# Even layer: the second heads' logarithms in one row on ScalarE, their operands at slab eleven, the sums over later keys one slab on, and two projections in borrowed PSUM banks

## The chip, the cores and the metric

The kernel runs on one core of one Trainium2 chip. The metric is the device time of one execution in microseconds (us); lower is better. It is compared as the median over several executions.

## The reference, cut to what matters

The program is two small networks in a row over 256 tokens of width 1024, all in float32. The first is one gated recurrent block with an expert layer. The second has two layers; each is an FFN, a mixer and an FFN with residuals. The mixer of the even layer is the stage that the change is about; the odd layer's mixer (16 heads over blocks of 256 keys) is touched in one place.

```python
def even_mixer(h, w_in, w_pool, pool_scale, w_out):
    proj = h @ w_in                                   # 1024 -> 2048
    q, k, v, u = jnp.split(proj, [512, 1024, 1536], axis=-1)
    a = stick_breaking_attention(q, k, v by 8 heads of 64)
    p = multiscale_pool(u, w_pool, pool_scale)
    return jnp.concatenate([merge_heads(a), p], axis=-1) @ w_out

# stick_breaking_attention, per head and block of 128 queries
z = q @ k.T / 8
past = spos < tpos
log_1m = where(past, log_sigmoid(-z), 0)
later = cumsum(log_1m, axis=keys, reverse=True) - log_1m
a = where(past, exp(log_sigmoid(z) + later), 0)
out = a @ v
```

In front of every FFN and mixer stands `rmsnorm`: x is divided by the root of its mean square per token and scaled by a gain.

## The kernel before

**Weights.** All weights come as one stream of slabs (128 x 1024 float32, 512 KB) through a ring of four buffers. Each slab passes three engines: SyncE loads `raw`, ScalarE rounds it to `w_hi` (`split_hi`, line 559), VectorE subtracts to get `w_lo` (`split_lo`, line 939). Slab n + 4 can be split only when TensorE has used slab n. TensorE multiplies every weight tile three times (hi x hi, lo x hi, hi x lo), so a slab is 24 matmuls.

**Norm.** The product of a projection is linear in x, so TensorE starts with the unscaled operand (`h_hi`, `h_lo`), and `rstd`, the reciprocal root, is multiplied in when a tile is read out. Its own chain is: squares, a matmul with ones (`norm`, PE), `Sqrt` (`root`, ScalarE), `RECIPROCAL` (line 962, VectorE). In `even_in` and `qkv`, `norm` is issued after slab 1.

**Projection.** `project` puts slab i of a stage into `tile_buf(j)`, which alternates between two buffers of the PSUM tensor `tile`. `free_tile(j)` makes PE wait until the reader of tile j - 2 (VectorE's `take`, or ScalarE) is done. So slab 2 of `even_in` and of `qkv` waits for the first `take`, and that one for `rstd`.

**Even layer.** `even_in` has 16 slabs. By a permutation of the stream, slabs 0 to 7 are q and k of a pair of heads each, 8 to 11 are the four groups of u for the pooling, and 12 to 15 are v, taken in pairs by `project_tokens` (48 matmuls each, slabs 12 and 13, then 14 and 15; the reader is ScalarE's `take_v`). The attention is done in two groups g of four heads:

- `head_scores(pair)` on PE, after slabs 3, 5, 7 and 8, writes z into `banks`, four PSUM banks that are FFN accumulators (`acc`) in other stages; ScalarE copies them to `az` (line 840).
- `ln_one_plus(g)` on ScalarE: Abs (814), Exp (816), Ln (818). Exp and Ln need different function tables, and each change of table is an `ACT_TABLE_LOAD`. Group 0 has its steps at slabs 5 and 6, group 1 at slabs 8, 9 and 10, one each, with a `split_hi` between.
- `stick_L_of(g)` on VectorE: `asp` (1469), the masked operand `aL` (1471) that PE waits for, `az - asp` (1474).
- `later_sums(g)` on PE: 16 matmul instructions, four heads into the four `banks`. Group 0 comes after slab 9, group 1 after slab 11. Group 1 writes the banks of group 0, so each of its heads waits until VectorE has read that of group 0 (`stick_w`).
- `stick_logs(g)` on VectorE (1481) reads those banks; `stick_exp(g)` on ScalarE (825) and `stick_shares(g)` on VectorE (1487) end with the weights `az`.
- `window_means(0..3)` on VectorE (1500 to 1505) is the pooling.

Each engine runs the order in which its own block of code is written. VectorE does, per slab, `take`, then `split_lo` of the slab four on. Before the `split_lo` of slab 12 + 4 it has one long block: logs of group 0, operands of group 1, shares of group 0, window means and logs of group 1 in turn. After the projections, PE multiplies the pooled values (it waits for the last `take_v`), forms the attention outputs, and starts `even_out` when `y_lo` is ready (`y`, line 1531, is the first step to it on VectorE).

**Odd layer.** `qkv` starts in the same way (slabs 0, 1, `norm`, slabs 2, 3, `turn_rstd`, `head_scores(0)`); its head scores use banks 0 and 1 only.

Of the kernel before, what the change touches and what calls it, by code (L numbers as in the profile page):

```python
# [29 lines left out]
T = 256  # L30
# [78 lines left out]
POOL_SLABS, EVEN_V = 8, 12  # L109
# [58 lines left out]
def build(nc, stream, x_in, cols_in, ones_in, keys_in, wpool_in, mixc_in, attc_in, out):  # L168
    first, NSLAB = stream_plan()
    readers = tile_readers(first)  # L170
    tile_at = {}
# [22 lines left out]

    def tile_buf(j, half=0):

        return tile[:, 2 * (j % 2) + half, :]

    def pair_buf(c, tt):
# [3 lines left out]
    def reads(engine, j):  # L203

        return sum(r == engine for r in readers[:j + 1])

    with ExitStack() as ctx:
# [109 lines left out]
        tile = ctx.enter_context(nc.psum_tensor("tile", [P, 4, T], F32))  # L317
        banks = acc[:, :, :].rearrange("p (b a) t -> p b (a t)", b=4)
        fronts = front[:, :, :]


        landed = [sem(f"slab_landed{i}") for i in range(RING)]
# [3 lines left out]
        slab_used = sem("slab_used")  # L326
        pool_done = sem("pool_products_done")
        tile_read = {"act": sem("tile_read_by_act"), "dve": sem("tile_read_by_dve")}
# [208 lines left out]
        def _(act):  # L537
# [247 lines left out]
            for kind, i in layer_stages():  # L785
# [21 lines left out]
                elif kind == "even":  # L807
                    def ln_one_plus(g, steps):

                        of = slice(4 * g, 4 * g + 4)  # L810
                        for step in steps:
                            if step == 0:
                                act.wait_ge(z_read, 4 * g + 4)
                                link(nc.scalar.activation(asp[:, of, :], az[:, of, :], ACT.Abs))
                            elif step == 1:
                                link(nc.scalar.activation(asp[:, of, :], asp[:, of, :], ACT.Exp, scale=-1.0))
                            else:
                                nc.scalar.activation(asp[:, of, :], asp[:, of, :], ACT.Ln, bias=1.0)\
                                    .then_inc(ln_ready, 1)

                    def stick_exp(g):

                        a, b = 4 * g, 4 * g + 4
                        act.wait_ge(stick_w, b)
                        nc.scalar.activation(az[:, a:b, :], az[:, a:b, :], ACT.Exp).then_inc(stick_e, 1)

                    n = first["even_in"]
                    for i in range(16):
                        if i == EVEN_V:
                            stick_exp(0)  # L830
                            stick_exp(1)
                        act.wait_ge(slab_used, n + i + 1)
                        if i >= EVEN_V and i % 2:
                            take_v("even_in", i - 1, i - 1 - EVEN_V, av)
                        split_hi(n + i + RING)
                        if i in STICK_AFTER:
                            pair = STICK_AFTER[i]
                            for h in (2 * pair, 2 * pair + 1):
                                act.wait_ge(z_done, h + 1)
                                nc.scalar.activation(az[:, h, :], banks[:, h % 4, 0:3 * P], ACT.Copy,  # L840
                                                     scale=SCALE).then_inc(z_read, 1)
                        if i == 5:
                            ln_one_plus(0, range(2))
                        elif i == 6:
                            ln_one_plus(0, [2])
                        elif i in (8, 9, 10):
                            ln_one_plus(1, [i - 8])
                    act.wait_ge(tile_read["dve"], reads("dve", tile_at["pooled"] + 3))
                    nc.scalar.copy(y_hi[:, 4:8, :], y32[:, 4:8, :]).then_inc(y_hi_ready, 1)
                    for g in range(2):  # L850
# [73 lines left out]
        def _(dve):  # L924
# [516 lines left out]
            for at, (kind, i) in enumerate(stages):  # L1441
# [18 lines left out]
                elif kind == "even":  # L1460
# [4 lines left out]
                    def stick_L_of(g):  # L1465

                        a, b = 4 * g, 4 * g + 4
                        dve.wait_ge(ln_ready, g + 1)
                        link(nc.vector.scalar_tensor_tensor(asp[:, a:b, :], az[:, a:b, :], 0.0,
                                                            asp[:, a:b, :], ALU.max, ALU.add))  # L1470
                        nc.vector.tensor_tensor(aL[:, a:b, :], asp[:, a:b, :],
                                                past_neg.unsqueeze(1).broadcast_to([P, 4, 3 * P]),
                                                ALU.mult).then_inc(stick_L, 1)
                        link(nc.vector.tensor_tensor(az[:, a:b, :], az[:, a:b, :], asp[:, a:b, :],
                                                     ALU.subtract))

                    def stick_logs(g):

                        for h in range(4 * g, 4 * g + 4):
                            dve.wait_ge(later_done, h + 1)  # L1480
                            nc.vector.tensor_tensor(az[:, h, :], banks[:, h % 4, 0:3 * P], az[:, h, :],
                                                    ALU.add).then_inc(stick_w, 1)

                    def stick_shares(g):
                        a, b = 4 * g, 4 * g + 4
                        dve.wait_ge(stick_e, g + 1)
                        nc.vector.scalar_tensor_tensor(az[:, a:b, :], az[:, a:b, :], -1.0,
                                                       past_neg.unsqueeze(1).broadcast_to([P, 4, 3 * P]),
                                                       ALU.mult, ALU.mult).then_inc(stick_a, 1)

                    def window_means(g):

                        src = pu[:, g, :]
                        if g == 0:
                            dve.wait_ge(tile_read["dve"], reads("dve", tile_at["even_in"] + POOL_SLABS + 3))
                        else:
                            dve.wait_ge(pooled_ready, g)
                        for r in range(g + 1):
                            to = win[:, r % 2, :]
                            link(nc.vector.tensor_tensor(to[:, PAD:], src[:, PAD:],  # L1500
                                                         src[:, PAD - 2 ** r:PAD - 2 ** r + T], ALU.add))
                            src = to
                        link(nc.vector.tensor_tensor(src[:, PAD:], src[:, PAD:], inv_count[:, g, :],
                                                     ALU.mult))
                        nc.vector.tensor_tensor(pooled[:, g, :], src[:, PAD:], pu[:, g, PAD:],
                                                ALU.subtract).then_inc(pooled_ready, 1)

                    n = first["even_in"]
                    for i in range(16):
                        if i == 4:  # L1510
                            r_columns(2)
                        if i < POOL_SLABS:
                            take("even_in", i, (ak if i % 2 else aq)[:, i // 2, :])
                        elif i < EVEN_V:
                            take("even_in", i, pu[:, i - POOL_SLABS, PAD:PAD + T])
                        if i == EVEN_V:
                            stick_logs(0)
                            stick_L_of(1)
                            stick_shares(0)
                            window_means(0)  # L1520
                            window_means(1)
                            stick_logs(1)
                            window_means(2)
                            stick_shares(1)
                            window_means(3)
                        split_lo(n + i + RING)
                        if i == 8:
                            stick_L_of(0)
                    dve.wait_ge(pool_done, 4)
                    for g in range(4):  # L1530
                        nc.vector.tensor_scalar(y32[:, 4 + g, :], tile[:, g, :],
# [85 lines left out]
        def _(pe):  # L1617
# [11 lines left out]
                return mm(out, lo, r_hi, False, stop, **kw)  # L1629

            def free_tile(j):
                if j >= 2:
                    r = readers[j - 2]
                    pe.wait_ge(tile_read[r], reads(r, j - 2))

            def project(name, i, n, hi, lo, lows=None, ks=range(KT), parts={}):

# [301 lines left out]
            for kind, i in layer_stages():  # L1939
# [5 lines left out]
                elif kind == "even":  # L1945
# [30 lines left out]
                    for i in range(16):  # L1976
                        if i < EVEN_V:
                            project("even_in", i, n + i, h_hi, h_lo, lows if i == 0 else None)
                        elif i % 2 == 0:
                            project_tokens("even_in", i, i - EVEN_V, n + i, h_hi, h_lo)  # L1980
                        if i == 1:
                            norm(q - 1)
                        elif i == 3:
                            turn_rstd(q - 1)
                        if i in STICK_AFTER:
                            head_scores(STICK_AFTER[i])
                        if i == 9:
                            later_sums(0)
                        elif i == 11:
                            later_sums(1)  # L1990
# [162 lines left out]
```

## Time and profile before

| | |
|---|---|
| median of 3 executions | 2194.0 us (2191.49 to 2195.93) |
| profiled execution, its own time | 2195.41 us |
| its span | 2193.4 us |
| busy in the span: PE / VectorE / ScalarE | 2059.9 (94%) / 1476.1 (67%) / 1079.0 us (49%) |
| mean granted TensorE clock | 0.977 |
| stage of the even mixer (`even_in` to the start of `even_out`) | 1363.3 to 1449.1 us |
| start of `qkv` to the start of `w_o` | 1861.4 to 1963.7 us |

The span is what the trace covers; the time of the execution is 2.0 us longer. The profiled execution lies 1.4 us above the median. A row of the timeline gives start and duration in us, engine, line, operation, and in brackets how long the engine had been idle and which instruction released it.

### The profile page before, as it was taken

Reading aid. Unit: us, or ns where it says so; the run is one execution under the profiler, and the core shown is the slowest. Engines: PE = TensorE matmul, PEld = TensorE weight load, DVE = VectorE, ACT = ScalarE, POOL = GpSimd, SP = SyncE. Lnnn points to the kernel's source line nnn. Section 1 sums busy time; section 2 is a strip of 40 time slices with the busy share of each in tenths; the row PEclk is TensorE's granted clock in tenths of the full one; section 3 lists DMA queues with packets and bytes.
Section 4 is the critical chain, followed back from the end, with each engine's and each line's share of the span. In section 5 each row is a group of like instructions: output and inputs, shape, how many; then the busy total and the mean of one; then the engine's idle time right before and its main releaser. Section 6 shows DMA issues by size and latency. Waiting matters only on the chain.

```text
span 2193.4 us, 42453 instructions
## 1 busy us (share of the span) xinstructions
PE 2059.9 (94%) x15492; PEld 1953.6 (89%) x15492; DVE 1476.1 (67%) x2393; ACT 1079.0 (49%) x1659; POOL 55.4 (3%) x36
## 2 busy tenths in 40 slices
PE   7899967899999999999998999799999999999997
PEld 7898865689999999999998999689999999889997
DVE  5687699966666666666666556676556556856555
ACT  5445326944444444444445444544445444555443
POOL 0000240000000000000000000000000000000000
PEclk9899998999999999999999999999999999999999
DMA  5344430045555555555555555335555565335552
GB/s 195 120 135 146 152 116 1 0 156 187 184 191 185 187 183 191 189 184 184 189 188 168 186 174 170 125 106 188 186 174 171 181 185 180 126 125 173 183 187 100
DMA packets 95683, 348.19 MB, mean 159 GB/s; under 512 B 10752, under 2 KB 10880, under 8 KB 95360
## 3 DMA queue, kind: packets, MB, share of 16 engines
q1 hardware_dynamic: 95184, 344.88, 48.3%
q10 hardware_dynamic: 432, 2.36, 0.3%
q8 instruction: 48, 0.79, 0.1%
q14 instruction: 19, 0.16, 0.0%
HBM read 346.15 MB, written 1.05 MB: 158 GB/s over the span
## 4 chain that ended last, share of the span: by engine, by line
PE 81%; DVE 12%; ACT 4%; issue 2%; DVEq 0%; DMA 0%; ACTq 0%; SPq 0%
PE front L1619 39%; PE acc L1619 29%; PE tile L1619 12%; DVE w_lo L939 2%; DVE pick L1392 2%; ACT w_hi L559 2%; DVE pick L1386 1%; DVE rstd L962 1%; DVE h_lo L969 1%; DVE chosen L1368 0%; DVE x L1450 0%; DVE rest L1283 0%; DVE top_i L1279 0%; DVE top_i L1297 0%; DVE top_v L1275 0%
## 5 line engine op out<-in xcount | busy, mean ns | idle before, releaser
L939 DVE TENSOR_TENSOR w_lo<-raw,w_hi 128x1024 fp32r<-128x1024 f32 x636 | 778.2, 1224 | 188.4 <-ACT w_hi L559 188.1
L559 ACT CAST w_hi<-raw 128x1024 fp32r<-128x1024 f32 x652 | 680.5, 1044 | 360.1 <-PE front L1619 144.4
L1619 PE MATMUL front<-h_hi,w_hi 128*128 128x256 f32 x2432 | 690.2, 284 | 8.2 <-DVE h_lo L969 7.5
L1619 PE MATMUL front<-h_hi,w_lo 128*128 128x256 f32 x2432 | 689.0, 283 | 0.0
L1619 PE MATMUL front<-h_lo,w_hi 128*128 128x256 f32 x2432 | 688.9, 283 | 0.0
L1619 PEld LDWEIGHTS front<-h_hi,w_hi 128*128 128x128 f32 x2432 | 466.9, 192 | 15.1 <-DVE h_lo L969 5.4
L1619 PEld LDWEIGHTS front<-h_lo,w_hi 128*128 128x128 f32 x2432 | 467.0, 192 | 5.0
L1619 PEld LDWEIGHTS front<-h_hi,w_lo 128*128 128x128 f32 x2432 | 467.0, 192 | 0.0
L608 ACT ACTIVATE scaled<-scaled 128x256 f32<-128x256 f32 x216 | 90.2, 418 | 500.6 <-DVE scaled L1024 289.0
L1019 DVE TENSOR_TENSOR scaled<-front,rstd 128x512 f32<-128x512 f32 x88 | 60.8, 691 | 275.9 <-PE front L1619 275.8
L1619 PE MATMUL tile<-h_hi,w_hi 128*128 128x256 f32 x736 | 219.8, 299 | 23.0 <-DVE h_lo L1082 4.9
L1619 PE MATMUL tile<-h_lo,w_hi 128*128 128x256 f32 x736 | 213.5, 290 | 0.0
L1619 PE MATMUL tile<-h_hi,w_lo 128*128 128x256 f32 x736 | 213.2, 290 | 0.0
L1619 PE MATMUL acc<-w_hi,mid_hi 128*128 128x512 f32 x512 | 201.9, 394 | 2.8 <-DVE mid_lo L1038 2.8
L1619 PE MATMUL acc<-mid_hi,w_hi 128*128 128x256 f32 x704 | 200.0, 284 | 4.2 <-DVE mid_lo L1038 4.2
L1619 PE MATMUL acc<-w_hi,mid_lo 128*128 128x512 f32 x512 | 201.3, 393 | 0.0
L1619 PE MATMUL acc<-w_lo,mid_hi 128*128 128x512 f32 x512 | 199.7, 390 | 0.0
L1619 PE MATMUL acc<-mid_lo,w_hi 128*128 128x256 f32 x704 | 199.3, 283 | 0.0
L1619 PE MATMUL acc<-mid_hi,w_lo 128*128 128x256 f32 x704 | 199.2, 283 | 0.0
L1619 PEld LDWEIGHTS tile<-h_hi,w_hi 128*128 128x128 f32 x736 | 146.5, 199 | 29.2 <-issue 7.8
L1619 PEld LDWEIGHTS tile<-h_lo,w_hi 128*128 128x128 f32 x736 | 146.8, 199 | 0.3 <-issue 0.2
L1619 PEld LDWEIGHTS tile<-h_hi,w_lo 128*128 128x128 f32 x736 | 146.5, 199 | 0.0
(254 smaller groups left out, 2622.0 us busy)
## 6 DMA issues: line engine op xcount, KB each, us to landing
raw<-stream SPq DMA_DIRECT2D x652, 512.0 KB, 3.5
x<-x_t SPq DMA_DIRECT2D x2, 512.0 KB, 4.8
keysT<-keys_t ACTq DMA_DIRECT2D x1, 1024.0 KB, 5.5
attc<-attention_constants ACTq DMA_DIRECT2D x1, 1024.0 KB, 5.6
out_t<-h SPq DMA_DIRECT2D x4, 256.0 KB, 2.2
mixc<-mixer_constants SPq DMA_DIRECT2D x1, 704.0 KB, 9.2
wpool<-w_pool ACTq DMA_DIRECT2D x1, 256.0 KB, 7.0
lane<-lanes SPq DMA_DIRECT2D x1, 128.0 KB, 4.8
```

The lines of the kernel that those rows point to most:

```text
L559: nc.scalar.copy(w_hi[:, s, :], raw[:, s, :]).then_inc(hi_ready, 1)
L608: nc.scalar.activation(scaled[:, k, 0:T], scaled[:, k, 0:T], func).then_inc(gate_ready, 1)
L939: nc.vector.tensor_tensor(w_lo[:, s, :], raw[:, s, :], w_hi[:, s, :].bitcast(F32), ALU.subtract).then_inc(lo_ready, 1)
L962: nc.vector.reciprocal(rstd[:, :], rstd[:, :]).then_inc(rstd_ready, 1)
L969: nc.vector.scalar_tensor_tensor(h_lo[:, k, :], x[:, k, :], col(gain, k), h_hi[:, k, :].bitcast(F32), ALU.mult, ALU.subtract)\
L1019: nc.vector.tensor_tensor(scaled[:, k, :].rearrange("p (a t) -> p a t", a=2), fronts[:, k, :].rearrange("p (a t) -> p a t", a=2), r, ALU.m ...
L1386: nc.vector.tensor_tensor(rows, iota.unsqueeze(1).broadcast_to([P, 3, P]), idx1_T[:, t(1, 3)].unsqueeze(2).broadcast_to([P, 3, P]), ALU.is ...
L1392: nc.vector.tensor_tensor(pick2[:, half, :, :], iota.unsqueeze(1).broadcast_to([P, 4, P]), idx2_T[:, t].unsqueeze(2).broadcast_to([P, 4, P ...
L1619: return nc.tensor.matmul(out, lhsT, rhs, start=start, stop=stop, **kw)
```

## The change

Five edits in one kernel:

1. In `even_in` and `qkv`, slabs 2 and 3 are projected into banks 2 and 3 of `banks` in place of `tile`, with no wait for a reader. Slabs 4 and 5, which use `tile` again, wait for the readers of slabs 0 and 1.
2. On ScalarE the three steps of `ln_one_plus(1)` all stand at slab 8, with no `split_hi` between.
3. On PE `later_sums(0)` comes after slab 10, not 9.
4. On VectorE `stick_L_of(1)` and then `stick_logs(0)` stand after the `split_lo` of turn 10 (slab 14), ahead of `take` of slab 11. In the block at slab 12 the order becomes means 0 and 1, shares 0, logs 1, means 2 and 3, shares 1.
5. On ScalarE `stick_exp(1)` is issued after the wait for slab 12, not before.

```diff
     def tile_buf(j, half=0):
+        for name in ("even_in", "qkv"):
+            if name in first and 2 <= j - tile_at[name] < 4:
+                return borrowed[j - tile_at[name]]
         return tile[:, 2 * (j % 2) + half, :]
...
+        borrowed = {i: banks[:, i, 0:T] for i in (2, 3)}
...
                         if i == EVEN_V:
                             stick_exp(0)
+                        act.wait_ge(slab_used, n + i + 1)
+                        if i == EVEN_V:
                             stick_exp(1)
-                        act.wait_ge(slab_used, n + i + 1)
...
-                        elif i in (8, 9, 10):
-                            ln_one_plus(1, [i - 8])
+                        elif i == 8:
+                            ln_one_plus(1, range(3))
...
                         if i == EVEN_V:
-                            stick_logs(0)
-                            stick_L_of(1)
-                            stick_shares(0)
                             window_means(0)
                             window_means(1)
+                            stick_shares(0)
                             stick_logs(1)
                             window_means(2)
+                            window_means(3)
                             stick_shares(1)
-                            window_means(3)
                         split_lo(n + i + RING)
                         if i == 8:
                             stick_L_of(0)
+                        elif i == 10:
+                            stick_L_of(1)
+                            stick_logs(0)
...
             def free_tile(j):
-                if j >= 2:
-                    r = readers[j - 2]
-                    pe.wait_ge(tile_read[r], reads(r, j - 2))
+                before = 2
+                for name in ("even_in", "qkv"):
+                    if name in first and 2 <= j - tile_at[name] < 4:
+                        return
+                    if name in first and 4 <= j - tile_at[name] < 6:
+                        before = 4
+                if j >= before:
+                    r = readers[j - before]
+                    pe.wait_ge(tile_read[r], reads(r, j - before))
...
-                        if i == 9:
+                        if i == 10:
                             later_sums(0)
                         elif i == 11:
                             later_sums(1)
```

**PE at the start of `even_in`.** The rows begin with `norm` (the matmul of `sq` with ones in `lane`); what follows is slab 2. Before, then of the change:

```order
L1619 MATMUL front<-sq,lane 128x256 [waits norm_squares_added]
L1619 MATMUL tile<-h_hi,w_hi 128x256 [waits slab_lo_ready,tile_read_by_dve]
L1619 MATMUL tile<-h_lo,w_hi 128x256
L1619 MATMUL tile<-h_hi,w_lo 128x256
L1619 MATMUL tile<-h_hi,w_hi 128x256
```

```order
L1625 MATMUL front<-sq,lane 128x256 [waits norm_squares_added]
L1625 MATMUL acc<-h_hi,w_hi 128x256 [waits slab_lo_ready]
L1625 MATMUL acc<-h_lo,w_hi 128x256
L1625 MATMUL acc<-h_hi,w_lo 128x256
L1625 MATMUL acc<-h_hi,w_hi 128x256
```

The target is now `acc`, and the wait for VectorE's reader is gone; the same holds for slab 3 and for both in `qkv`.

**VectorE from `take` of slab 9 on** (`pu` is u of the pooling). Before, then of the change:

```order
L991 TENSOR_TENSOR pu<-tile,rstd 128x256 [waits slab_used,dve_own_steps]
L939 TENSOR_TENSOR w_lo<-raw,w_hi 128x1024 [waits slab_hi_ready]
L991 TENSOR_TENSOR pu<-tile,rstd 128x256 [waits slab_used]
L939 TENSOR_TENSOR w_lo<-raw,w_hi 128x1024 [waits slab_hi_ready]
L991 TENSOR_TENSOR pu<-tile,rstd 128x256 [waits slab_used]
L939 TENSOR_TENSOR w_lo<-raw,w_hi 128x1024 [waits slab_hi_ready]
L1481 TENSOR_TENSOR az<-acc,az 128x384 [waits stick_later_done] x4
L1469 SCALAR_TENSOR_TENSOR asp<-az,asp 128x1536 [waits stick_ln_ready]
L1471 TENSOR_TENSOR aL<-asp,attc 128x1536 [waits dve_own_steps]
L1474 TENSOR_TENSOR az<-az,asp 128x1536
L1487 SCALAR_TENSOR_TENSOR az<-az,attc 128x1536 [waits stick_exp_ready,dve_own_steps]
```

```order
L996 TENSOR_TENSOR pu<-tile,rstd 128x256 [waits slab_used,dve_own_steps]
L944 TENSOR_TENSOR w_lo<-raw,w_hi 128x1024 [waits slab_hi_ready]
L996 TENSOR_TENSOR pu<-tile,rstd 128x256 [waits slab_used]
L944 TENSOR_TENSOR w_lo<-raw,w_hi 128x1024 [waits slab_hi_ready]
L1474 SCALAR_TENSOR_TENSOR asp<-az,asp 128x1536 [waits stick_ln_ready]
L1476 TENSOR_TENSOR aL<-asp,attc 128x1536 [waits dve_own_steps]
L1479 TENSOR_TENSOR az<-az,asp 128x1536
L1486 TENSOR_TENSOR az<-acc,az 128x384 [waits stick_later_done,dve_own_steps]
L1486 TENSOR_TENSOR az<-acc,az 128x384 [waits stick_later_done] x3
L996 TENSOR_TENSOR pu<-tile,rstd 128x256 [waits slab_used]
L944 TENSOR_TENSOR w_lo<-raw,w_hi 128x1024 [waits slab_hi_ready]
```

The operands `aL` and then the logs of group 0 have moved up by one `take` and one `split_lo`, and the logs now follow the operands.

**ScalarE from the Abs of group 1 on.** Before, then of the change:

```order
L814 ACTIVATE asp<-az 128x1536 [waits stick_z_read]
L559 CAST w_hi<-raw 128x1024 [waits slab_landed3,slab_used,act_own_steps]
L816 ACT_TABLE_LOAD
L816 ACTIVATE asp<-asp 128x1536
L559 CAST w_hi<-raw 128x1024 [waits slab_landed0,slab_used,act_own_steps]
L818 ACT_TABLE_LOAD
L818 ACTIVATE asp<-asp 128x1536
L559 CAST w_hi<-raw 128x1024 [waits slab_used,slab_landed1]
```

```order
L818 ACTIVATE asp<-az 128x1536 [waits stick_z_read]
L820 ACT_TABLE_LOAD
L820 ACTIVATE asp<-asp 128x1536 [waits act_own_steps]
L822 ACT_TABLE_LOAD
L822 ACTIVATE asp<-asp 128x1536 [waits act_own_steps]
L563 CAST w_hi<-raw 128x1024 [waits slab_used,slab_landed3]
L563 CAST w_hi<-raw 128x1024 [waits slab_used,slab_landed0]
L563 CAST w_hi<-raw 128x1024 [waits slab_used,slab_landed1]
```

The number of instructions and of table loads is the same; the casts of slabs 13 and 14, each of which waits for a slab to be used, now stand behind the Ln.

## Rows read from the trace of the kernel before

**Rows 1.** The page, section 4: chain that ended last, by engine

```profile
PE 81%; DVE 12%; ACT 4%; issue 2%; DVEq 0%; DMA 0%; ACTq 0%; SPq 0%
```

**Rows 2.** Timeline, TensorE alone: first matmuls after a pause

```profile
1374.76 0.39 PE L1619 MATMUL tile<-h_hi,w_hi 128*128 128x256 f32 x1 [2.89 <-DVE aq L991]
...
1405.34 0.91 PE L1619 MATMUL acc<-aL,attc 128*128 128x384 f32 x2 [2.92 <-DVE aL L1471]
...
1423.48 1.65 PE L1619 MATMUL acc<-aL,attc 128*128 128x384 f32 x2 [8.65 <-DVE aL L1471]
...
1874.15 0.39 PE L1619 MATMUL tile<-h_hi,w_hi 128*128 128x256 f32 x1 [2.81 <-DVE bq L993]
```

**Rows 3.** Chain that ended last, in order of time: start, us, what

```profile
1366.76 4.68 PE tile L1619 x36
1371.44 0.45 PE front L1619 x2
...
1374.76 6.03 PE tile L1619 x48
...
1405.34 3.74 PE acc L1619 x16
...
1423.48 6.01 PE acc L1619 x16
1429.49 11.52 PE tile L1619 x96
...
1864.84 6.07 PE tile L1619 x36
...
1874.15 7.51 PE tile L1619 x48
```

**Rows 4.** Stretches: PE, PEld, DVE, ACT, POOL busy (count), PEclk, DMA share, GB/s

```profile
1415.00:1424.00 9.00, 0.52 (x1) 0.50 (x2) 7.37 (x9) 4.62 (x4) 0.00 (x0) 0.66 0.36 118
...
1430.00:1442.00 12.00, 10.99 (x92) 10.79 (x90) 10.28 (x18) 5.11 (x6) 0.00 (x0) 1.00 0.11 36
...
1874.00:1882.00 8.00, 7.85 (x52) 7.68 (x54) 4.64 (x7) 1.27 (x2) 0.00 (x0) 0.79 0.43 131
...
1890.00:1942.00 52.00, 52.00 (x446) 49.04 (x445) 42.72 (x108) 33.60 (x86) 0.00 (x0) 1.00 0.43 142
```

**Rows 5.** Timeline, ScalarE: Abs, Exp and Ln of group 1

```profile
1401.37 1.49 ACT L814 ACTIVATE asp<-az 128x1536 f32<-128x1536 f32 x1
1402.89 1.04 ACT L559 CAST w_hi<-raw 128x1024 fp32r<-128x1024 f32 x1
1403.95 1.28 ACT L816 ACT_TABLE_LOAD   x1
1405.24 1.48 ACT L816 ACTIVATE asp<-asp 128x1536 f32<-128x1536 f32 x1
...
1414.43 1.49 ACT L818 ACTIVATE asp<-asp 128x1536 f32<-128x1536 f32 x1
```

**Rows 6.** Timeline, VectorE, in the even layer and one row of the odd

```profile
1401.74 1.75 DVE L1469 SCALAR_TENSOR_TENSOR asp<-az,asp 128x1536 f32<-128x1536 f32 x1
...
1406.99 0.42 DVE L991 TENSOR_TENSOR pu<-tile,rstd 128x256 f32<-128x256 f32 x1
...
1418.03 1.94 DVE L1481 TENSOR_TENSOR az<-acc,az 128x384 f32<-128x384 f32 x4
1419.89 1.75 DVE L1469 SCALAR_TENSOR_TENSOR asp<-az,asp 128x1536 f32<-128x1536 f32 x1
...
1425.13 1.76 DVE L1487 SCALAR_TENSOR_TENSOR az<-az,attc 128x1536 f32<-128x1536 f32 x1
...
1438.23 2.35 DVE L939 TENSOR_TENSOR w_lo<-raw,w_hi 128x1024 fp32r<-128x1024 f32 x2
...
1445.00 1.65 DVE L1531 TENSOR_SCALAR y<-tile,cols 128x256 f32<-128x256 f32 x4
...
1878.82 0.42 DVE L993 SCALAR_TENSOR_TENSOR bq<-tile,rstd 128x256 f32<-128x256 f32 x1 [2.13 <-PE tile L1619]
```

## The prediction

> **What bounds the kernel now.** I read the chain that ended last first: TensorE holds 81% of it, VectorE 12%, ScalarE 4% [rows 1]. So time is won where PE stands still, or where it runs at half rate. The timeline of PE gives the places that the change touches [rows 2]: four pauses, of 2.89, 2.92 and 8.65 us in the even layer and 2.81 us in `qkv`. The first and the last are released by the first `take` (`aq`, `bq`), which waits for `rstd`; the two others by `aL`, the operand of `later_sums(0)` and `later_sums(1)`. The chain in order of time gives what PE's pieces cost at either rate [rows 3]: 48 matmuls take 6.03 us in the even layer but 7.51 us behind the pause in `qkv`, and the 16 instructions of the sums 3.74 us for group 0 but 6.01 us for group 1. The stretches say why [rows 4]: the granted clock is 0.66 around the pause of 8.65 us and 0.79 from 1874 to 1882 us, that is, part of the time at 1.2 instead of 2.4 GHz; from 1430 on it is 1.00 again.
>
> All times below are on the clock of the trace of before, so that they can be compared with its rows.
>
> **Borrowed banks, even layer.** Slab 1 ends at 1366.76 + 4.68 = 1371.44, `norm` takes 0.45, and PE then stands until 1374.76 [rows 2, 3]. With slabs 2 and 3 in banks of their own it goes on at about 1371.8: a gain of 3.0 us. Their weights were split before the `RECIPROCAL`, so nothing holds them. Slab 4 now waits for the first `take`, which the old slab 2 already had at 1374.7; it comes up at about 1378.9. ScalarE's row up to the Abs of group 1 hangs on PE's slabs and moves by the same 3.0.
>
> **ScalarE's row.** Abs starts at 1401.37 - 3.0 = 1398.4. Abs, load, Exp, load, Ln are 1.49 + 1.28 + 1.48 + 1.28 + 1.49 = 7.0 us [rows 5], so Ln ends at 1405.4 (before: 1414.43 + 1.49 = 1415.9). The price is the cast of slab 13, 1.04 us, now behind it: done at 1406.45, where the old one, moved by 3.0, would have ended at 1400.9. Nobody on PE needs slab 13 before slab 12's turn, but VectorE stands at its `w_lo`: `stick_L_of(0)` starts at 1401.74 - 3.0 = 1398.7, and `take` of slab 9 is over at 1407.4 - 3.0 = 1404.4 [rows 6]. So VectorE idles 2.05 us there. I count that in full. In the rows ScalarE's Exp starts 0.01 us after the end of its load (1403.95 + 1.28 against 1405.24) [rows 5]. The Trainium skill (ScalarE: Activation LUTs, What ACT_TABLE_LOAD costs) adds to a load of about 1.28 us a drain of about 1.38 us; by that the two loads in a row would end Ln 2.8 us later. The trace has the load and no room for the drain; that case is the third rival.
>
> **`later_sums(0)` one slab on.** PE ends slab 9 at 1405.34 - 2.92 - 3.0 = 1399.4. It used to stand for `aL` here. Now slab 10 (a quarter of 11.52, so 2.9 us) fills the time to 1402.3, and `aL` of group 0 is ready 3.55 us after 1398.7, at 1402.3. The pause of 2.92 us goes. The sums run to about 1406.0, slab 11 (its tile's reader was through at 1404.4) to 1408.8.
>
> **Operands and logs at slab eleven.** VectorE from 1406.45: `w_lo` 13 (1.2), `take` (0.4), `w_lo` 14 (1.15; a pair takes 2.35) to 1409.2 [rows 6]. Then `stick_L_of(1)`, which takes 1425.13 - 1419.89 = 5.25 us, to 1414.4, and the logs of group 0, 1.86 us from 1418.03 to 1419.89 [rows 6], to 1416.3. PE's sums of group 1 now wait for the first of these logs, at 1414.9 to 1415.0. PE stands 6.2 us in place of 8.65. **This is the wait that takes the place of the one removed**: no longer `aL`, but the reading of bank 0. Queued behind it are slabs 12 to 15 and the attention outputs.
>
> **To the end of the stage there are two bounds.** (a) VectorE: `take` and `w_lo` 15 to 1417.8; the block at slab 12 was without a pause from 1418.03 to 1438.23, and without logs 0 and operands 1 it is the 13.1 us from 1425.13 to 1438.23: 1430.9. Four `w_lo` at half of 2.35 each: 1435.6. Then `y` starts, before at 1445.00: 9.4 us earlier [rows 6]. Putting means 3 ahead of shares 1 costs nothing in this sum, since the attention outputs come after the pooled products on PE. (b) PE: sums from 1415.0, at the half rate as before 6.0 us, to 1421.0; slabs 12 to 15 in 11.52 us to 1432.5. Before they ended at 1429.49 + 11.52 = 1441.0 and `y` started 4.0 us later; so `y` at 1436.5, 8.5 us earlier. With the sums at full rate (3.74 us) PE would be through at 1430.2, and (a) binds. The pause of 6.2 us lies between that of 2.9, after which the sums ran at full rate, and that of 8.65, after which they didn't; it is nearer to the longer one, and I take 8.5. `stick_exp(1)` behind the wait for slab 12 is done by 1428.5, and shares 1 want it at 1429.2: nothing. **Even layer: 8.5 us, ends 8.5 and 9.4.**
>
> **Borrowed banks, odd layer.** Slab 1 ends at 1864.84 + 6.07 = 1870.9, and `norm` takes 0.45 [rows 3]: PE goes on at 1871.35 instead of 1874.15, 2.8 us. Without the pause I expect the 48 matmuls in 6.0 instead of 7.51 us, another 1.5: **4.3 us, ends 2.8 and 4.5.** VectorE must follow. It stood 2.13 us at 1878.82 for PE, the first of several such waits up to the first scores, so it can begin earlier with PE. Afterwards it is busy 42.72 of 52.00 us against PE's 52.00 [rows 4, 6], which leaves room to catch up the rest.
>
> **Sum.** 8.5 + 4.3 = 12.8 us. `even_out`, the FFNs and `w_o` are only shifted: each slab there waits for work that has moved too. The number of instructions is the same. The profiled execution would come from 2195.4 to 2182.6 us; it lay 1.4 above the median, and from the median of 2194.0 it is **2181.2 us**. The bounds of the two parts, 11.3 and 13.9, give 2180.1 to 2182.7; medians may differ by 1.5 to 2, as the executions shown spread over 4.4 us. The likeliest case's own range is 2178 to 2184.5.
>
> **The rivals.**
> 1. *The odd layer gives nothing.* VectorE paces `qkv`, and PE's head start is taken back by tiles that are read no earlier. For it: VectorE has the most work in the layer after PE. Against it: its pause of 2.13 us, and its 9.3 idle us of 52. Only 8.5 would be left: 2185.5 us. 7%.
> 2. *The wait for bank 0 is longer.* VectorE comes 2.5 us later to the logs (a cast of slab 14 that waits, a `take` that waits), and PE stands 8.65 us as before. Then sums to 1423.4, slabs to 1434.9, `y` at 1438.9: 6.1 in the even layer, 2183.6 us. 5%.
> 3. *Loads back to back cost more.* If each of the two loads were followed by as much again (1.28 us), Ln and all behind it on VectorE would be 2.6 us late, `y` at 1438.2: 6.8 us, 2182.9 us. The page's drain makes it 2.8 us, so 2183.1. 3%.
> 4. *Slower: the half rate stays.* The pause of 6.2 us lies before 96 matmuls of slabs 12 to 15 and the 192 of `even_out`. Each costs 0.12 us more at half rate. If it holds over slabs 12 to 15 that is 11.5 us and leaves 1.3; from there on every slab of `even_out` costs up to 2.9 more, so it turns to slower from the first of them, and with all eight it is 11.5 + 23 - 12.8 = 22 us slower, 2216 us. For it: the half rate does follow the long pause. Against it: in the old trace, behind a longer pause, it ended with the sums: slabs 12 to 15 took 11.52 us, the full rate [rows 3]. The Trainium skill (TensorE: Matmul & The Clock Gate, What's actually happening) says that activity releases the throttle; the 1.00 of the stretch 1430 to 1442 agrees [rows 4]. 2%.
> 5. *Given back.* A wait for a load or a cast, or half rate in another place, takes over 8 us back: 2190 to 2194 us, no difference. I see no place for it. 5%.
>
> **How the numbers follow.** My forecast has 78%. It and rivals 1 to 3 are faster by over 0.2% (4.4 us, about what a measurement of this kernel can tell from no change): 93%, of which I give 2 to a half rate elsewhere: 0.91. Same: 0.06. Slower: 0.03. The range of 2177.5 to 2187 holds the likeliest case and rivals 1 to 3.
>
> **What would show it.** PE has no pause at slab 2 of either stage; none before `later_sums(0)`, or under 0.5 us; one of 5.5 to 7 us before `later_sums(1)`, now released by the logs (`az`) instead of `aL`; `even_out` starts 85.8 - 8.5 = 77.3 us after slab 0 of `even_in`; `qkv` to `w_o` takes 98.0 instead of 102.3 us. VectorE idles about 2 us at `w_lo` of slab 13. I am wrong if PE's pause at slab 2 comes back at slab 4 (the reader of slab 0 not through), if 48 matmuls after `norm` in `qkv` still take 7.5 us, or if `y` starts at 1438 or later.

## The result, and the profile after

| | before | changed |
|---|---|---|
| median | 2194.68 us (4 executions) | 2179.26 us (4: 2178.68 to 2180.28) |
| ratio | | 0.9932, 95% interval 0.9915 to 0.995 |
| profiled execution | 2195.41 us, span 2193.4 | 2179.39 us, span 2177.2 |
| even stage (slab 0 to the start of `even_out`) | 85.85 us | 76.84 us |
| odd stage (slab 0 of `qkv` to the start of `w_o`) | 102.22 us | 95.82 us |
| all the rest of the span | 2005.3 us | 2004.5 us |

The stage times are differences between the starts of first matmuls in the timeline. The kernel is 15.4 us faster by these medians. Two later measurements of the same kernel, each beside the kernel before on one chip, gave 2182.10 against 2194.51 (ratio 0.9941, 0.9927 to 0.9954) and 2181.17 against 2193.86 (0.9942, 0.9929 to 0.9956): 12.4 and 12.7 us. The forecast was 12.8 less, 2181.2.

Timeline of the changed kernel, TensorE alone, first matmuls after a pause (the rows that answer to [rows 2]):

```profile
1363.99 0.38 PE L1625 MATMUL tile<-h_hi,w_hi 128*128 128x256 f32 x1 [0.37 <-DVE h_lo L974]
...
1412.05 1.62 PE L1625 MATMUL acc<-aL,attc 128*128 128x384 f32 x2 [6.02 <-DVE az L1486]
...
1431.16 1.99 PE L1625 MATMUL tile<-pooled,wpool 128*128 128x256 f32 x8 [1.95 <-ACT av L595]
```

Of the four pauses three are gone, those at slab 2 in both layers and the one before `later_sums(0)`. The one of 8.65 us is now 6.02 us, and its releaser has changed from `aL` to `az` L1486, the logs of group 0. The chain of the changed kernel, in order of time (as [rows 3]):

```profile
1363.99 4.68 PE tile L1625 x36
1368.68 0.43 PE front L1625 x2
1369.11 5.75 PE acc L1625 x48
...
1412.05 5.66 PE acc L1625 x16
1417.71 11.52 PE tile L1625 x96
...
1854.53 4.68 PE tile L1625 x36
1859.22 0.43 PE front L1625 x2
1859.65 5.75 PE acc L1625 x48
```

Slabs 2 and 3 (48 matmuls into `acc`) follow `norm` at once, 5.75 us in either layer. Only the sums of group 1 still start at half rate; "at half rate" here and below means that part of the matmuls runs at the lower clock (5.66 us for 3.74). The stretch around them has a granted clock of 0.52, the next but one 1.00:

```profile
1409.00:1415.00 6.00, 2.95 (x6) 1.94 (x7) 5.97 (x9) 1.48 (x1) 0.00 (x0) 0.52 0.10 41
...
1421.00:1433.00 12.00, 10.05 (x77) 9.45 (x75) 11.06 (x17) 6.82 (x9) 0.00 (x0) 1.00 0.20 61
```

ScalarE's timeline of the changed kernel (as [rows 5]) and VectorE's (as [rows 6]):

```profile
1395.45 1.49 ACT L818 ACTIVATE asp<-az 128x1536 f32<-128x1536 f32 x1
1396.95 1.28 ACT L820 ACT_TABLE_LOAD   x1
1398.24 1.49 ACT L820 ACTIVATE asp<-asp 128x1536 f32<-128x1536 f32 x1
1399.75 1.28 ACT L822 ACT_TABLE_LOAD   x1
1401.04 1.48 ACT L822 ACTIVATE asp<-asp 128x1536 f32<-128x1536 f32 x1
```

```profile
1403.49 1.23 DVE L944 TENSOR_TENSOR w_lo<-raw,w_hi 128x1024 fp32r<-128x1024 f32 x1 [2.00 <-ACT w_hi L563]
1404.64 0.42 DVE L996 TENSOR_TENSOR pu<-tile,rstd 128x256 f32<-128x256 f32 x1
1404.97 1.22 DVE L944 TENSOR_TENSOR w_lo<-raw,w_hi 128x1024 fp32r<-128x1024 f32 x1
1406.10 1.75 DVE L1474 SCALAR_TENSOR_TENSOR asp<-az,asp 128x1536 f32<-128x1536 f32 x1
...
1411.35 1.95 DVE L1486 TENSOR_TENSOR az<-acc,az 128x384 f32<-128x384 f32 x4
...
1427.90 3.73 DVE L944 TENSOR_TENSOR w_lo<-raw,w_hi 128x1024 fp32r<-128x1024 f32 x3
1432.08 1.23 DVE L944 TENSOR_TENSOR w_lo<-raw,w_hi 128x1024 fp32r<-128x1024 f32 x1 [0.45 <-ACT w_hi L563]
1433.22 1.65 DVE L1537 TENSOR_SCALAR y<-tile,cols 128x256 f32<-128x256 f32 x4
```

The row Abs to Ln takes 7.07 us, and each activation starts 0.01 us after its load ends. VectorE idles 2.00 us for the cast of slab 13, as summed (2.05).

One place outside the two stages got slower. In the FFN behind `even_out` 36 matmuls took 6.11 us, against 4.69 before, at a granted clock of 0.72 for 1.00. No edit touches this code:

```profile
1669.72 4.69 PE front L1619 x36
```

```profile
1657.98 6.11 PE front L1625 x36
```

The first row is before, the second the changed kernel. The other two traces of the changed kernel have 5.82 and 6.10 us there.

### The profile page after: what moved, and what is told of

Same layout as the page of the kernel before. It is cut to its first block, busy times and chain, and to the rows that moved or that the text cites. A ratio compares the mean times of both kernels' runs of the same rounds, so it can differ in the third digit from the quotient of the medians.

```text
span 2177.2 us, 42448 instructions
## 1 busy us (share of the span) xinstructions
PE 2054.6 (94%) x15492; PEld 1949.7 (90%) x15492; DVE 1476.0 (68%) x2393; ACT 1079.1 (50%) x1659; POOL 55.4 (3%) x36
## 4 chain that ended last, share of the span: by engine, by line
PE 81%; DVE 10%; ACT 6%; issue 3%; ACTq 0%; DMA 0%; DVEq 0%; SPq 0%
PE front L1625 39%; PE acc L1625 30%; PE tile L1625 12%; DVE w_lo L944 2%; ACT w_hi L563 1%; ACT pick L727 1%; ACT G L734 1%; DVE h_lo L974 1%; DVE chosen L1373 0%; DVE rstd L967 0%; DVE rest L1288 0%; DVE top_i L1284 0%; DVE x L1455 0%; DVE top_i L1302 0%; DVE top_v L1280 0%
## 5 line engine op out<-in xcount | busy, mean ns | idle before, releaser
L1625 PEld LDWEIGHTS front<-h_hi,w_hi 128*128 128x128 f32 x2432 | 467.8, 192 | 15.4 <-DVE h_lo L974 5.8
L1625 PE MATMUL tile<-h_hi,w_hi 128*128 128x256 f32 x704 | 208.0, 296 | 17.0 <-DVE h_lo L1087 4.9
L1625 PE MATMUL tile<-h_lo,w_hi 128*128 128x256 f32 x704 | 201.8, 287 | 0.0
L1625 PE MATMUL tile<-h_hi,w_lo 128*128 128x256 f32 x704 | 201.6, 286 | 0.0
L1625 PEld LDWEIGHTS tile<-h_hi,w_hi 128*128 128x128 f32 x704 | 137.8, 196 | 22.3 <-issue 7.6
L1625 PEld LDWEIGHTS acc<-mid_hi,w_hi 128*128 128x128 f32 x704 | 135.1, 192 | 5.7 <-DVE mid_lo L1043 5.7
L1625 PEld LDWEIGHTS tile<-h_lo,w_hi 128*128 128x128 f32 x704 | 138.0, 196 | 0.3 <-issue 0.2
```

The source lines that it names most:

```text
L1625: return nc.tensor.matmul(out, lhsT, rhs, start=start, stop=stop, **kw)
```

## The experiments

Each kernel was timed beside the kernel before on its chip. The stage times come from one trace each and repeat closely for the changed kernel: even stage 76.84, 76.82 and 76.84 us, odd stage 95.82, 96.27 and 95.84. The rest of the span, code that no experiment touches, lay between 2001.7 and 2007.1 us in the fourteen traces. So the stages tell the small effects apart, not the medians. The odd stage is the rougher of the two: with the same code in it, it took 102.22 us before and 99.53 in order alone.

| kernel | median us | ratio to before, 95% | even | odd |
|---|---|---|---|---|
| banks alone | 2186.76 | 0.9967 (0.9955 to 0.9979) | 83.80 | 95.82 |
| order alone | 2186.38 | 0.9963 (0.9949 to 0.9977) | 81.34 | 99.53 |
| changed, banks in the even layer only | 2184.20 | 0.9955 (0.9941 to 0.9968) | 76.89 | 100.83 |
| changed, ScalarE's steps apart | 2180.43 | 0.9931 (0.9917 to 0.9944) | 75.68 | 96.91 |
| the same again | 2180.55 | 0.9935 (0.9921 to 0.9948) | 76.14 | 96.27 |
| changed, sums 0 after slab 9 | 2183.06 | 0.9951 (0.9937 to 0.9965) | 80.40 | 95.98 |
| changed, VectorE's old order | 2183.19 | 0.9952 (0.9939 to 0.9966) | 79.64 | 96.03 |
| tokens first | 2180.09 | 0.9939 (0.9926 to 0.9953) | 77.66 | 97.10 |
| tokens first, pooling on GpSimd | 2178.84 | 0.9933 (0.9919 to 0.9946) | 76.97 | 95.88 |
| operands first | 2177.29 | 0.9927 (0.9913 to 0.9940) | 75.15 | 96.27 |

**The changed kernel again**, twice, as the measure for the others.

> The changed kernel again, beside the three below on one chip. Expected: its even stage (slab 0 to the start of even_out) 76.8 us as in its first trace, within 0.3, and 48 matmuls behind norm in both layers in 5.75 to 6.0 us; median 2178.5 to 2180.5.

> The changed kernel once more, as the measure for the three below: even stage 76.8 us within 0.2; its median between 2179 and 2183, since the rest of the program varied by some 2 us between its first two traces.

Both as expected, but for the first median of 2182.10 (2180.07 to 2182.53), which lies above the window given: its trace has 2006.7 us for the rest against 2004.5 in the first trace.

**Banks alone**: the kernel before with the two edits to `tile_buf` and `free_tile`.

> Only the borrowed banks, in both layers; the order in the even layer is as before. Theory (parts add up): the pause of 2.9 us at slab 2 of the even layer goes and everything behind it moves by 3.0; in the odd layer the pause of 2.8 us goes and the half rate behind it too (2.8 to 4.4). Together 5.8 to 7.4 us faster than before, 2187 to 2189. Rival (the even layer is set by VectorE's long block, so an earlier slab 2 only lengthens the pause for the operands of group 1): nothing in the even layer, 2.8 to 4.4 us faster, about 2191; PE's pause before the sums of group 1 grows from 8.65 to over 11 us.

6.7 us faster. The pause for the operands of group 1 stays exactly 8.65, so the rival is out: the whole even layer moves with slab 2. The stage is only 2.05 us shorter, though, not 3.0, since the sums of group 0 now run at half rate behind their pause (5.22 us for 3.74 before), of which the sums of group 1 give 0.4 back (5.64 for 6.01). Chain of this kernel:

```profile
1369.59 5.75 PE acc L1623 x48
...
1399.88 5.22 PE acc L1623 x16
...
1419.50 5.64 PE acc L1623 x16
```

**Order alone**: the changed kernel without those edits.

> The changed kernel without the borrowed banks: only the new order in the even layer. Theory: the even layer gets 5.5 to 6.1 of its 9.0 us, the odd layer nothing: 5.5 to 6 us faster than before, about 2188.5. Pauses of 2.9 us at slab 2 in both layers, none before the sums of group 0, about 6 us before the sums of group 1, released by the logs. Rival (the two parts need each other): under 3 us.

7.1 us faster, and 6.7 + 7.1 = 13.8, against 12.4 to 15.4 us for the whole. Either interval reaches some 3 us to each side, so this says that neither part needs the other, and no more. In the even stage the parts give 2.05 + 4.51 = 6.6 us and the whole 9.0, because each part alone leaves a pause with slow matmuls behind it (1.5 us in banks alone, 1.35 here). The pauses are the expected ones. The even stage is 4.5 us shorter instead of 5.5 to 6.1, because here the 48 matmuls behind the pause at slab 2 run at half rate:

```profile
1372.82 7.38 PE tile L1622 x48
...
1417.41 5.13 PE acc L1622 x16
```

The odd stage is 2.7 us shorter than before although nothing in it has changed: 36 matmuls of slabs 0 and 1 took 4.68 us for 6.07, and 24 matmuls of the last attention outputs 1.53 for 2.83, each behind the same wait as before (0.4 and 3.33 us).

```profile
1960.84 2.83 PE acc L1619 x24
```

```profile
1954.14 1.53 PE acc L1622 x24
```

**Banks in the even layer only.**

```diff
-        for name in ("even_in", "qkv"):
+        for name in ("even_in",):
...
-                for name in ("even_in", "qkv"):
+                for name in ("even_in",):
```

> The changed kernel with the borrowed banks in the even layer only. Theory (the odd layer's share is the pause of 2.8 us and the half rate behind it): 2.8 to 4.4 us slower than the changed kernel, about 2183; PE pauses 2.8 us at slab 2 of the odd layer. If the 48 matmuls behind that pause take about 7.5 us, the half rate belongs to the pause, if 6.0, it was chance. Rival (the difference of 16 us between the two profiles was mostly the banks in the odd layer, whose stage came out 6.4 us shorter): 6 us or more slower.

The odd stage takes 100.83 us, 4.6 to 5.0 more than in the three traces of the changed kernel, and the even stage the same as there. By the medians it is 2 to 5 us slower. The pause and the matmuls behind it:

```profile
1863.45 0.39 PE L1625 MATMUL tile<-h_hi,w_hi 128*128 128x256 f32 x1 [2.81 <-DVE bq L998]
```

```profile
1863.45 7.50 PE tile L1625 x48
```

With the pause the 48 matmuls took 7.51, 7.49 and 7.50 us (before, order alone, this kernel), without it 5.74 or 5.75 in every trace where I read them. So the half rate belongs to the pause, and the change saves 2.81 + 1.75 = 4.6 us here.

**ScalarE's steps apart**, run twice.

```diff
-                        elif i == 8:
-                            ln_one_plus(1, range(3))
+                        elif i in (8, 9, 10):
+                            ln_one_plus(1, [i - 8])
```

> The changed kernel with ScalarE's Abs, Exp and Ln of group 1 apart again at slabs 8, 9 and 10, the casts of slabs 13 and 14 between them. Theory (the row in one piece costs VectorE a wait of 2.0 us for the cast of slab 13, and the Ln isn't wanted before 1404.6 on the clock of the changed kernel's trace): VectorE starts the operands of group 1 at 1404.6 instead of 1406.1, PE's pause before the sums of group 1 falls from 6.0 to 4.5 us, the kernel is 1 to 1.6 us faster than the changed one, about 2178. Rival (the row is what lets the operands of group 1 be ready early): slower than the changed kernel by 1 us or more, and VectorE waits for the Ln.

> ScalarE's steps apart again, now beside the changed kernel. Theory: even stage 75.7 us, 1.1 less than the changed kernel's, so its median 0.5 to 2 us lower. Rival (the gain in the stage is given back behind it): equal medians, with a longer rest of the program in both of its traces.

PE's pause falls to 4.66 and 4.65 us, the even stage to 75.68 and 76.14. The sums of group 1 took 5.89 us in the first trace and 6.35 in the second, which is the whole difference between the two stages; in the changed kernel they took 5.66. VectorE has no wait for slab 13, and a short one for the Ln:

```profile
1405.96 1.22 DVE L944 TENSOR_TENSOR w_lo<-raw,w_hi 128x1024 fp32r<-128x1024 f32 x1
1407.81 1.76 DVE L1474 SCALAR_TENSOR_TENSOR asp<-az,asp 128x1536 f32<-128x1536 f32 x1 [0.62 <-ACT asp L822]
```

So the logarithms in a row, the edit that gives the change its name, cost 0.7 to 1.2 us in the stage. Beside the changed kernel the medians, 2180.55 and 2181.17, don't separate the two.

**Sums of group 0 after slab 9 again.**

```diff
-                        if i == 10:
+                        if i == 9:
                             later_sums(0)
```

> The changed kernel with later_sums(0) after slab 9 again. Theory (a pause that is filled is worth nothing by itself: what counts is that slab 10 is used earlier, so that ScalarE's cast and VectorE's w_lo of slab 14 ahead of the operands of group 1 aren't late): PE stands about 2.9 us for the operands of group 0, slab 10 ends 6.5 us later, VectorE reaches the operands of group 1 about 2.2 us later, and PE's pause before the sums of group 1 becomes about 5 us: the even stage takes about 79.0 us, 2.2 more than the changed kernel's. Rival 1 (the pause of 2.9 us counts in full): 2.9 us more. Rival 2 (the longer pause later just shrinks by as much): no difference.

The stage is 3.56 us longer, and the forecast of 2.2 was too low; by the number alone rival 1 (2.9) is nearer. The path is the one of the theory, though. Counted from slab 0, slab 10 ended 8.1 us later, not 6.5, because the sums of group 0 ran at half rate behind their pause (5.16 us for 3.74), a term I had left out; and VectorE came to the operands of group 1 3.7 us later, not 2.2. The value of the edit is in two parts: slab 10 is used earlier, so its successor's cast isn't late, and the sums run at full rate.

```profile
1399.03 1.65 PE L1625 MATMUL acc<-aL,attc 128*128 128x384 f32 x2 [2.92 <-DVE aL L1476]
...
1415.36 1.62 PE L1625 MATMUL acc<-aL,attc 128*128 128x384 f32 x2 [5.42 <-DVE az L1486]
```

**VectorE's old order** in the changed kernel.

```diff
                         if i == EVEN_V:
+                            stick_logs(0)
+                            stick_L_of(1)
+                            stick_shares(0)
                             window_means(0)
                             window_means(1)
-                            stick_shares(0)
                             stick_logs(1)
                             window_means(2)
-                            window_means(3)
                             stick_shares(1)
+                            window_means(3)
...
-                        elif i == 10:
-                            stick_L_of(1)
-                            stick_logs(0)
```

> The changed kernel with VectorE's old order: logs of group 0 and operands of group 1 in the block at slab 12, means 3 last. Theory: the sums of group 1 start 1.7 to 1.8 us later than in the changed kernel, and shares 1 then waits for stick_exp(1), which now stands behind slab 12: some 2.4 us of idle VectorE; even stage 79.0 to 79.6, against 76.8. Rival 1 (only the operand's time counts): 78.5. Rival 2 (VectorE's work is the same in any order): 76.8 to 77.2.

79.64, 2.8 us more, at the upper edge of what the theory had (79.6): the pause becomes 7.79 us and is released by `aL` again, and shares 1 waits for the Exp behind slab 12. That wait needs edit 5, which stays in here; no run undoes edits 4 and 5 together, so what edit 4 is worth by itself stays open.

```profile
1429.96 1.76 DVE L1492 SCALAR_TENSOR_TENSOR az<-az,attc 128x1536 f32<-128x1536 f32 x1 [2.83 <-ACT az L829]
```

**Tokens first**: steps apart as above, and:

```diff
                         elif i == 10:
                             stick_L_of(1)
+                        elif i == 11:
                             stick_logs(0)
...
-                        elif i == 11:
+                        elif i == 12:
                             later_sums(1)
```

> From the kernel with ScalarE's steps apart: logs of group 0 one turn later on VectorE (after take and w_lo of turn 11), and the sums of group 1 on PE after slabs 12 and 13. It fills PE's pause. Theory (VectorE's block now sets the end of the stage): PE's pause before the sums falls from 4.7 to under 1 us, slabs 12 to 15 end some 2.5 us earlier, yet y starts only about 0.5 us earlier: even stage about 75.2 us against 75.7. Rival (PE still sets the end): 2 us or more earlier.

A miss: 77.66 us, 1.5 to 2 more than its parent. The pause didn't shrink, it moved: 4.48 us, now ahead of slab 12, which waits for the `take` of slab 11 behind the operands. I had still written "under 1 us". The half rate that followed hit 48 matmuls (8.40 for 5.76 us). The sums of group 1 behind them then came late for VectorE, which stood 1.65 us for the first and three times 0.31 for the others before it could take the logs:

```profile
1411.01 8.40 PE tile L1626 x48
1419.41 3.48 PE acc L1626 x16
```

```profile
1420.32 0.56 DVE L1486 TENSOR_TENSOR az<-acc,az 128x384 f32<-128x384 f32 x1 [1.65 <-PE acc L1626]
```

**Pooling on GpSimd**, from the kernel above: the 18 operations of `window_means` move to GpSimd, with a semaphore for its own steps.

```diff
+                if q == 3:
+                    pool.wait_ge(attc_sem, 32)
+                    for g in range(4):
+                        window_means(g)
...
                         if i == EVEN_V:
-                            window_means(0)
-                            window_means(1)
                             stick_shares(0)
                             stick_logs(1)
-                            window_means(2)
-                            window_means(3)
                             stick_shares(1)
```

> As the one before, and window_means on GpSimd, which takes 7.9 us out of VectorE's block. Theory (VectorE's block is the bound in the kernel before this one): y starts about 2 us earlier than there, even stage about 73 us, then PE's last slabs bound it; the kernel is 3 to 4 us faster than the changed one, about 2176. Rival (both engines slow each other down, or GpSimd is late with pooled): VectorE's operations of 128x1536 take over 1.76 us while GpSimd works, or PE waits for pooled; no gain or a loss.

76.97 us, 0.7 less than its parent instead of 2.2, and 4 us above the forecast of 73. GpSimd is in time with `pooled`, but the rival holds: while it works, VectorE's operations of 128 x 1536 take 2.17 to 2.30 us, alone 1.75; and GpSimd's own take 2.1 us beside those and 0.73 later. VectorE so comes to `take` of slab 11 2.1 us later after slab 0 than in the parent, and PE, which waits for it, stands 5.75 us:

```profile
1407.59 2.17 DVE L1504 TENSOR_TENSOR aL<-asp,attc 128x1536 f32<-128x1536 f32 x1
...
1416.97 1.76 DVE L1520 SCALAR_TENSOR_TENSOR az<-az,attc 128x1536 f32<-128x1536 f32 x1 [1.55 <-ACT az L857]
```

```profile
1408.23 2.12 POOL L542 TENSOR_TENSOR pooled<-win,pu 128x256 f32<-128x256 f32 x1
...
1421.58 0.73 POOL L542 TENSOR_TENSOR pooled<-win,pu 128x256 f32<-128x256 f32 x1
```

**Operands first**, from the changed kernel: ScalarE's Ln moves behind the cast of slab 13, and

```diff
+                        if i == 10:
+                            stick_L_of(1)
+                            stick_logs(0)
                         split_lo(n + i + RING)
                         if i == 8:
                             stick_L_of(0)
-                        elif i == 10:
-                            stick_L_of(1)
-                            stick_logs(0)
```

> From the changed kernel: the cast of slab 13 between Exp and Ln on ScalarE, and on VectorE operands 1 and logs 0 ahead of w_lo of slab 14. Theory: operands of group 1 start 2.5 us earlier, PE's pause before the sums of group 1 is 3.5 us, y starts 2.0 us earlier: even stage 74.8 us, median 1.5 to 2.5 us under the changed kernel's. Rival (w_lo of slab 14 late holds PE or the ring of slabs): PE pauses at slab 14 or VectorE waits for the cast of slab 18; stage 76 or more.

The pause is 3.57 us and the stage 75.15, 1.7 us under the changed kernel. The executions on the same chip, 2176.50 to 2179.09 us, don't overlap with the changed kernel's 2179.38 to 2181.76. It beats both kernels. The pause is 2.45 us shorter, but the sums behind it took 6.41 us for 5.66. The medians differ by 3.9 us, of which the two stages of its trace show only 1.2 to 1.7. Another 1.4 lie in the FFN behind `even_out`, where the 36 matmuls took 4.68 us here. Of the fourteen traces nine have 5.8 to 6.1 us at that place, all three of the changed kernel among them; before, tokens first, this kernel and both traces with the steps apart have 4.7. Whether the order of the kernel or chance decides this, no run shows.

```profile
1411.40 1.62 PE L1627 MATMUL acc<-aL,attc 128*128 128x384 f32 x2 [3.57 <-DVE az L1488]
```

## Why the prediction was right

- **Borrowed banks, even layer, 3.0 us**: right. PE went on 0.43 us after slab 1, and slab 4 found its tile free. In the trace of banks alone the pauses behind it were unchanged in length.
- **ScalarE's row**: the sum was right to 0.1 us, and so was its price on VectorE. The drain that the Trainium skill adds to a table load (ScalarE: Activation LUTs, What ACT_TABLE_LOAD costs) is not seen in the two loads in a row: 1.28 us each, and the activation follows. Rival 3 is out. What the prediction didn't say is that the edit was a loss. With the steps apart VectorE came to the operands at 1404.1, on the clock of the changed kernel's trace, and waited 0.62 us for the Ln; in the row the Ln is done at 1402.5, and VectorE comes only at 1406.1.
- **`later_sums(0)` one slab on**: the pause went. Its worth, read from the reverse, is 3.6 us. I had listed only the pause of 2.9, and neither slab 10 nor the half rate that can follow such a pause.
- **Operands and logs at slab eleven**: a pause of 6.2 us forecast, 6.02 found, with the releaser named. Reversed, with edit 5 left in, the order on VectorE costs 2.8 us.
- **Two bounds to the end**: the PE bound held, with the sums at half rate (5.66 us for 6.0). VectorE waited 0.45 us for the cast of slab 19, so its own bound was close behind. 9.0 us against 8.5, ends 8.5 and 9.4; the 0.5 are 0.3 in the sums and 0.2 in the pause. That the sums would run at half rate was chosen by comparing two pauses. One of them, 2.92 us with the full rate behind it, was a single case: behind the same pause the sums took 5.22 and 5.16 us in two later traces. So the choice was right, but its reason weak.
- **Odd layer, 4.3 us**: mis-sized a little. Pause and half rate are 4.6 us; I took 6.0 us for the 48 matmuls and they need 5.75. The pair of first traces shows 6.4, but 1.4 of that is no work of the change: slabs 0 and 1 of `qkv` ran at half rate in part in the trace of before (6.07 for 4.68 us), and so they did once with the change in place (6.08 in the first trace with the steps apart). Most of what is left, 0.5 us, are the 24 matmuls of the last attention outputs (2.37 us for 2.83).
- **The rest**: 0.8 us in the first pair of traces, inside its own scatter of some 5 us, most of it ahead of 440 us, where the clock varies between executions of the same code. The first measurement's 15.4 against 12.4 and 12.7 in the others is of that size, and I don't read more from it. The forecast said that all code behind the even stage is only shifted. The 36 matmuls in the FFN took 1.4 us more in the first trace, so that is not quite so. That 12.4 and 12.7 us come so near to 12.8 is therefore partly luck: the stages gave 0.5 and 0.3 us more than forecast, and about 1.4 went again behind them, by the one trace of before that there is.

Rival 1 (nothing in the odd layer) is out: PE had no pause in `qkv` up to the value slabs. Rival 4 (the half rate stays over slabs 12 to 15 and beyond) is out: slabs 12 to 15 took 11.52 us. Nor does it stay in tokens first, where slabs 12 and 13 lose 2.6 us right behind the pause and the sums after them take 3.48.

## What to carry to other kernels

Price a pause of TensorE with what runs behind it. A pause of some 3 us cost up to 1.75 us more in the matmuls that followed, and one of 3.6 us cost 2.7. Where it came, the loss was much the same for sums (1.4 to 2.7 us) and for slabs (1.3 to 2.6), and it wasn't free in either: between the two traces with the steps apart the sums differ by 0.46 us, and so do the stages.

When a wait is taken away, look for the instruction that frees the next resource. Here the worth of moving one group of matmuls lay in using a slab earlier, and thus in the cast that waits for it.

Of several edits that go in together, undo each one alone: one of the five here was worth less than nothing once the others were in. Edit 5 was never undone.

## What the runs showed of the hardware

- After a pause of 2.8 to 2.9 us the half rate is not certain. In `qkv`, 48 matmuls took 7.5 us behind it in three traces of three. In the even layer it was 6.03 us before and 7.38 in order alone; the sums of group 0 behind 2.92 us took 3.74 us before, 5.22 in banks alone and 5.16 in sums after slab 9.
- A longer pause did not mean a longer half rate. The sums of group 1, 3.74 us at full rate (as the sums of group 0 without a pause), took 6.41 us behind a pause of 3.57 (operands first), 5.89 and 6.35 behind 4.66 and 4.65, 5.66, 5.66 and 5.21 behind 6.02 to 6.04 (the changed kernel), and 6.01 and 5.64 behind 8.65 (before, banks alone).
- Several short waits in a row can be followed by half rate too. Ahead of the 36 matmuls in the FFN after `even_out` TensorE waited 0.9 us once, 0.5 twice and 0.4 twice, before and in the changed kernel alike; the 36 took 4.7 us in five and 5.8 to 6.1 in nine of fourteen traces.
- GpSimd and VectorE slow each other on SBUF tensors in float32: 128 x 1536 on VectorE from 1.75 to 2.17 or more, 128 x 256 on GpSimd from 0.73 to 2.12 us. VectorE's reads of PSUM (`take` 0.42 us, the logs 1.95) kept their times, and `w_lo` took 1.22 to 1.30 us, while GpSimd's additions beside it took 1.5 to 1.7 us for 0.61 alone.
- 48 matmuls took 5.75 us into the borrowed banks behind `norm`, and 5.94 or 5.95 into `tile` behind the eight matmuls of the head scores. It is not the target that makes the difference: into `tile` behind six matmuls to `front` they took 5.75 us too, in the same trace of the changed kernel.
